# Column sums on TensorE against one column of ones instead of 64, at three places of a tuned transformer kernel

## The chip, the cores and the metric

The kernel runs as one program on one core of a Trainium2 chip. The metric is the device time of one launch in microseconds, as the median of several runs. Lower is better.

## What is computed

A sequence of 512 tokens of width 1024 goes through three layers. Layer A mixes tokens with a gated delta net of six heads of 128, and also attends to a memory of 256 rows; layer B has stick-breaking attention of twelve heads in that place; layer C pools, does a difference of two softmax attentions for four heads, and a cross attention to a second memory. Each layer ends with an MLP of width 4096. The change touches three sums of squares inside the layers:

```python
q = l2norm(qkv[..., :W].reshape(B, S, H, Dh)) * (Dh ** -0.5)      # layer A, six heads
k = l2norm(qkv[..., W:2 * W].reshape(B, S, H, Dh))                # layer A, six heads
...
o = o * lax.rsqrt(jnp.mean(o * o, axis=-1, keepdims=True) + EPS) * o_gain      # layer A, six heads
...
o = rms_norm_2(o, g_subln[l]) * (1.0 - lam_init)                  # layer C, four heads of 128
```

Each is one number per token and head: the sum of 128 squares.

## The kernel before, in words

Activations lie transposed: a head is a tile of 128 partitions (its features) by 512 tokens. A weight matrix comes in units of 1024 by 256 from DMA into `STG`, and ScalarE and VectorE split each unit into a high and a low part (`WH`, `WL`). TensorE multiplies high by high, high by low and low by high; these are the rows `HH,WH`, `HL,WH` and `HH,WL` of the profile. All engines follow an order written out by hand and meet through counting semaphores. TensorE's order is the function `_(pe)`, and every matmul of its helper `mm` shows as line 500.

A sum of squares over a head goes like this. ScalarE squares the head's tile (into `SQ`, or into `KDC`, which lies in the buffer `Y`). TensorE takes a block of 128 tokens of the squares as the stationary operand and streams columns of ones through it; the result in PSUM has the 128 tokens on partitions, and each streamed column gives the same sum. With `[:, 0:64]` the sum is written 64 times side by side, and the next block's result starts one column further and writes over 63 of them. In the end the columns from the first one on hold one sum per block, and VectorE reads only those.

The three places:

- `beside_gate(n)`, n from 0 to 5, lies between and behind the two tiles of each of three gate units of layer A. Each call does two of the twelve heads of queries and keys, four blocks each. Heads 0 to 5 of its order go to columns from 0 of PSUM bank 6, heads 6 to 11 to columns from 256. VectorE reads them at lines 2518 (`decays_2`) and 2540 (`decays_4`).
- `norm_sums(g, bank)` does three heads of the delta net's output, twelve blocks. `norm_sums(0, 7)` lies in the triangular inversion of the second group of heads (`between_1`, step 1), `norm_sums(1, 4)` beside the output projection of layer A (`norms_beside`).
- `head_sums(h)` in `out_between_heads` does one head of layer C, four blocks: one call ahead of `tile_k(0)` of the output projection, three behind it.

Other sums of the kernel, in `sum_tokens`, have the same form with one column of ones:

```python
mm(PS[:, 4, b:b + 1], blk(SQA[:, :], b), con("ones")[:, 0:1], b == 0, False, skip_group_check=True)
```

At four places between layers, `finish_post` runs two and then five matmuls whose results nobody reads (`keep_running`, rows `WH`), one set ahead of `spread_tokens` and one behind it.

Of the kernel before, what the change touches and what calls it, by code (L numbers as in the profile page):

```python
# [27 lines left out]
ALU = mybir.AluOpType  # L28
# [3 lines left out]
P = 128  # L32
# [3 lines left out]
NB = S // P  # L36
# [6 lines left out]
EPS = 1e-6  # L43
# [70 lines left out]
def program(nc, ws, xt_in, memt_in, memt2_in, par_in, con_in, rope_in, rcnt_in, out):  # L114
    ctx = ExitStack()
    with ctx:
        def sb(name, shape, dt=F32, scope=ctx, align=32):
            return scope.enter_context(nc.sbuf_tensor(name, shape, dt, align_bytes=align))
# [15 lines left out]
        SC = sb("SC", [P, H_LIN, 8, NB])  # L134
# [15 lines left out]
        SQ = sb("SQ", [P, 4, S])  # L150
# [9 lines left out]
        PS = ctx.enter_context(nc.psum_tensor("PS", [P, 8, 512], F32))  # L160
        PSF = PS[:, :, :].rearrange("p b n -> p (b n)")

        def con(name, width=P):
            return CON[:, CCOL[name]:CCOL[name] + width]
# [84 lines left out]
        KDC = [Y[:, 3 + e, :] for e in range(3)]  # L249
# [30 lines left out]
        def blk(ap, b, n=P):  # L280
            return ap[:, b * n:(b + 1) * n]
# [35 lines left out]
        def emptied(kind, u, j, i=None, step=0):  # L317

            return lin(EMPTIED[kind][u] + j + 1, 2 * step, i)
# [20 lines left out]
        def split_done(q, k):  # L340
            return 8 * SPLITS.index(q) + k + 1
# [154 lines left out]
        def _(pe):  # L496
            I_ = con("ident")

            def mm(o, l, r, start, stop, **kw):
                return pe.matmul(o, l, r, start=start, stop=stop, **kw)  # L500
# [26 lines left out]
            def wait_bank(u, j, i=None, step=0):  # L527

                if u >= 2:
                    kind = KIND[u - 2]  # L530
                    pe.wait_ge(sems[f"emptied_{kind}"], emptied(kind, u - 2, j, i, step))
# [494 lines left out]
            def norm_sums(g, bank):  # L1026

                pe.wait_ge(sems["osq"], 3 * g + 6)
                for e in range(3):
                    for b in range(NB):  # L1030
                        last = mm(PS[:, bank, NB * e + b:NB * e + b + 64], blk(KDC[e], b), con("ones")[:, 0:64], True, True)
                last.then_inc(sems["oss"], 1)

            def norm_rows(n, bank):
# [6 lines left out]
            def norms_beside(n):  # L1041
                if n == 1:
                    norm_sums(1, 4)
                if n == 3:
                    norm_rows(3, 2)
                    norm_rows(4, 3)
                    norm_rows(5, 4)
# [185 lines left out]
            def out_between_heads(u):  # L1233

                def tile_k(k):
                    pe.wait_ge(sems["hl"], split_done("C.mix", k))
                    for j in range(2):
                        bank = PS[:, 2 * (u % 2) + j, :]
                        wh, wl = WH[u % 2][:, k, j * P:(j + 1) * P], WL[u % 2][:, k, j * P:(j + 1) * P]
                        mm(bank, wh, HH[:, k, :], k == 0, False)  # L1240
                        mm(bank, wh, HL[:, k, :], False, False)
                        last = mm(bank, wl, HH[:, k, :], False, k == KD - 1)
                        if k == KD - 1:
                            last.then_inc(sems["tile"], 1)

                def head_sums(h):
                    pe.wait_ge(sems["df_sq"], h + 1)
                    for b in range(NB):
                        last = mm(PS[:, 7, NB * h + b:NB * h + b + 64], blk(SQ[:, h, :], b), con("ones")[:, 0:64], True, True)
                    if h == 3:  # L1250
                        last.then_inc(sems["df_ss"], 1)

                def head_factors(h):
                    for b in range(NB):
                        last = mm(PS[:, 4 + h, b * P:(b + 1) * P], COEF[:, NB * h + b:NB * h + b + 1].to_broadcast([P, P]),
                                  I_, True, True)
                    last.then_inc(sems["df_bc"], 1)

                pe.wait_ge(sems["emptied_act"], emptied("act", U0["C.mem"] + 7, 1))
                pe.wait_ge(sems["df_at"], 12)  # L1260
                pe.wait_ge(sems["lo"], u + 1)
                wait_bank(u, 0)
                wait_bank(u, 1)
                head_sums(0)
                tile_k(0)
                head_sums(1)
                head_sums(2)
                head_sums(3)
                tile_k(1)
                tile_k(2)  # L1270
                pe.wait_ge(sems["df_rs"], 3)
                head_factors(0)
                head_factors(1)
                tile_k(3)
                head_factors(2)
                head_factors(3)
                for k in range(4, KD):
                    tile_k(k)
# [26 lines left out]
            def beside_gate(n):  # L1305

                for t in (2 * n, 2 * n + 1):
                    pe.wait_ge(sems["l2sq"], t + 1)
                    if t == 6:
                        pe.wait_ge(sems["sc_dve"], 7)  # L1310
                    for b in range(NB):
                        c = NB * t + b if t < 6 else 256 + NB * (t - 6) + b
                        last = mm(PS[:, 6, c:c + 64], blk(SQ[:, t % 4, :], b), con("ones")[:, 0:64], True, True)
                    last.then_inc(sems["l2ss"], 1)
                if n == 0:
                    pe.wait_ge(sems["emptied_dve"], emptied("dve", U0["A.bg"], 1))
                    for b in range(NB):
                        last = pe.transpose(PS[:, 5, b * 12:(b + 1) * 12], blk(BGT[0:12, :], b), I_[0:12, 0:12])
                    last.then_inc(sems["bg_tr"], 1)
                if n == 3:  # L1320
                    mm(PS[:, 5, 64:88], con("tri_le"), SC[:, :, 0, :], True, True)
                    mm(PS[:, 5, 96:120], con("ones"), SC[:, :, 0, :], True, True).then_inc(sems["gc_mm"], 1)
                if n == 4:
                    pe.wait_ge(sems["rows_in"], 4)
                    pe.wait_ge(sems["sc_dve"], 10)
                    pe.wait_ge(sems["sc_act"], 7)
                    for ty in range(3):
                        last = pe.transpose(PS[0:64, 5, P + ty * P:2 * P + ty * P], ROWS_IN[:, ty, :], I_)
                    last.then_inc(sems["rows_tr"], 1)
# [5 lines left out]
            for r in range(NU["A.gate"]):  # L1335
                product(U0["A.gate"] + r, None, 0, HH, HL, between=lambda: beside_gate(2 * r),
                        beside=lambda n: memory_a(16 * r + n))
                beside_gate(2 * r + 1)
# [721 lines left out]
        def _(dve):  # L2060
# [3 lines left out]
            def tt(o, a, b, op):  # L2064
                return dve.tensor_tensor(o, a, b, op)  # L2065
# [418 lines left out]
            hb = lambda ap: ap.rearrange("p (h b) -> p h b", b=NB)  # L2484
            sm = [SMALL[:, r, :] for r in range(8)]
            step_ = [0]

            def sc(ins):

                step_[0] += 1  # L2490
                ins.then_inc(sems["sc_dve"], 1)
                dve.wait_ge(sems["sc_dve"], step_[0])
# [22 lines left out]
            def decays_2():  # L2515

                dve.wait_ge(sems["l2ss"], 6)
                sc(dve.tensor_scalar(sm[6], PS[:, 6, 0:24], EPS, None, ALU.add))
                sc(dve.reciprocal(sm[6], sm[6]))
                sc(tt(hb(sm[2]), SC[:, :, 1, :], hb(sm[6]), ALU.mult))  # L2520
                row = ROWS_IN[:, 2, :].rearrange("p (a n) -> p a n", a=2)[:, :, 0:24]
                dve.tensor_copy(row, sm[2].unsqueeze(1).to_broadcast([P, 2, 24])).then_inc(sems["rows_in"], 1)
# [14 lines left out]

            def decays_4():
                dve.wait_ge(sems["l2ss"], 12)
                sc(dve.tensor_scalar(SC[:, :, 3, :], hb(PS[:, 6, 256:280]), EPS, P * P * EPS, ALU.add, ALU.mult))  # L2540

            def gate_tile(u, i, step, j):
                t = 2 * (u - U0["A.gate"]) + j
# [4 lines left out]
            for r in range(NU["A.gate"]):  # L2548
# [17 lines left out]
                if r == 1:  # L2566
                    rows()
            decays_4()
            delta_net()
            for q, k in enumerate((3, 4, 5)):  # L2570
# [313 lines left out]
```

## Time and profile before

| what | value |
|---|---|
| runs of the kernel | 2172.91, 2175.64, 2178.26 us |
| median | 2175.64 us |
| time of the profiled execution | 2172.91 us |
| its span in the trace | 2171.1 us |
| granted TensorE clock, mean | 0.997 |
| TensorE matmul busy | 2110.8 us, 97% of the span |
| TensorE weight load busy | 1738.7 us, 80% |
| VectorE / ScalarE / GpSimd busy | 1082.4 / 746.4 / 178.9 us |
| DMA | 182.81 MB, 84 GB/s on average |

The span runs from the first to the last instruction; the profiled execution's own time is 1.8 us longer. PE is TensorE's matmuls, PEld its weight loads, which run ahead of the matmuls and beside them. The matmuls are pipelined, so their times overlap: the cost of a matmul in a row of many is the distance from its start to the next one's start, and not its duration. One fp32 matmul of the code appears as two matmuls with a weight load each in the trace; they are called passes here.

### The profile page before, as it was taken

How to read it: one execution, taken by the hardware profiler on the slowest of the kernel's cores; microseconds unless marked ns; L12 is line 12 of the kernel's file. 1: busy time of each engine (PE TensorE's matmuls, PEld its weight loads, DVE VectorE, ACT ScalarE, POOL GpSimd, SP SyncE). 2: the span in 40 equal slices, each digit the busy share in tenths (PEclk: the TensorE clock that was granted, in tenths of full speed). 3: DMA queues.
4: the chain of work that ended last, by engine and by line, in shares of the span. 5: the costliest groups of instructions: out<-in, count | busy, mean ns of one | idle time of the engine just before them, and what ended most of it. 6: DMA issues, size and time to landing. Idle time of an engine off the chain costs nothing.

```text
span 2171.1 us, 28830 instructions
## 1 busy us (share of the span) xinstructions
PE 2110.8 (97%) x11847; PEld 1738.7 (80%) x11847; DVE 1082.4 (50%) x1381; ACT 746.4 (34%) x1025; POOL 178.9 (8%) x145
## 2 busy tenths in 40 slices
PE   7999999999999999999999999999899999999998
PEld 7887788788888878767788888788688878888886
DVE  4764655455354453353645445455675345354453
ACT  6444433422122232574412222322464243222221
POOL 3000220300000220001300000311001000000001
PEclk9999999999999999999999999999999999999999
DMA  6231000232322222101222222232132202222221
GB/s 242 78 116 41 21 22 4 77 112 87 105 96 85 107 77 86 39 1 59 78 97 97 97 97 97 107 117 97 59 119 96 84 33 97 97 97 97 97 97 58
DMA packets 27025, 182.81 MB, mean 84 GB/s; under 512 B 2992, under 2 KB 3120, under 8 KB 5424
## 3 DMA queue, kind: packets, MB, share of 16 engines
q1 hardware_dynamic: 25776, 177.67, 23.2%
q0 software_dynamic: 432, 2.62, 0.3%
q8 instruction: 74, 1.21, 0.2%
q10 hardware_dynamic: 720, 1.11, 0.1%
q14 instruction: 23, 0.19, 0.0%
HBM read 179.30 MB, written 2.10 MB: 84 GB/s over the span
## 4 chain that ended last, share of the span: by engine, by line
PE 89%; DVE 6%; ACT 4%; DMA 1%; issue 1%; ACTq 0%; DVEq 0%
PE PS L500 88%; ACT Y L1389 2%; DVE Y L2062 1%; ACT WH L1389 1%; DVE WL L2065 1%; DVE Y L2065 1%; DMA MX<-mem_t 0%; DVE SQ L2065 0%; DMA STG<-weights 0%; PE PS L713 0%; DVE DMX L2676 0%; ACT ABUF L1389 0%; DVE HL L2065 0%; DVE HL L2062 0%; ACT SQ L1389 0%
## 5 line engine op out<-in xcount | busy, mean ns | idle before, releaser
L500 PE MATMUL PS<-HH,WH 128*128 128x512 f32 (+1 forms) x1608 | 631.7, 393 | 9.1 <-ACT HH L1389 4.3
L500 PE MATMUL PS<-HH,WL 128*128 128x512 f32 (+1 forms) x1608 | 619.9, 386 | 0.0
L500 PE MATMUL PS<-HL,WH 128*128 128x512 f32 (+1 forms) x1608 | 609.1, 385 | 0.0
L2065 DVE TENSOR_TENSOR WL<-STG,WH 128x2048 fp32r<-128x2048 f32 (+1 forms) x163 | 367.9, 2257 | 284.7 <-ACT WH L1389 284.6
L1389 ACT ACTIVATE WH<-STG 128x2048 fp32r<-128x2048 f32 (+2 forms) x171 | 314.9, 1841 | 523.8 <-PE PS L500 521.9
L500 PEld LDWEIGHTS PS<-HH,WH 128*128 128x128 f32 x1608 | 302.2, 188 | 85.3 <-issue 12.9
L500 PEld LDWEIGHTS PS<-HL,WH 128*128 128x128 f32 x1608 | 302.2, 188 | 61.4 <-issue 2.4
L500 PEld LDWEIGHTS PS<-HH,WL 128*128 128x128 f32 x1608 | 302.3, 188 | 59.5
L500 PE MATMUL PS<-UPH,WH 128*128 128x512 f32 x832 | 324.3, 390 | 1.4 <-DVE UPL L2062 1.4
L500 PE MATMUL PS<-UPH,WL 128*128 128x512 f32 x832 | 323.8, 389 | 0.0
L500 PE MATMUL PS<-UPL,WH 128*128 128x512 f32 x832 | 323.8, 389 | 0.0
L500 PEld LDWEIGHTS PS<-UPH,WH 128*128 128x128 f32 x832 | 156.2, 188 | 34.0 <-DVE UPL L2062 1.8
L500 PEld LDWEIGHTS PS<-UPL,WH 128*128 128x128 f32 x832 | 156.2, 188 | 32.4
L500 PEld LDWEIGHTS PS<-UPH,WL 128*128 128x128 f32 x832 | 156.2, 188 | 32.4
L423 POOL TENSOR_TENSOR SQA<-SQ 128x512 f32<-128x512 f32 (+1 forms) x14 | 24.2, 1728 | 1571.7 <-ACT SQ L1389 1571.7
L2062 DVE SCALAR_TENSOR_TENSOR RR<-PS,RS 128x512 f32<-128x512 f32 x96 | 66.3, 691 | 146.3 <-PE PS L500 138.4
L2065 DVE TENSOR_TENSOR Y<-Y,PS 128x512 f32<-128x512 f32 x64 | 44.0, 688 | 180.1 <-PE PS L500 180.1
L1389 ACT ACTIVATE UPH<-RR 128x512 fp32r<-128x512 f32 x64 | 40.5, 632 | 226.7 <-DVE RR L2062 226.7
L2065 DVE TENSOR_TENSOR XT<-XT,PS 128x512 f32<-128x512 f32 x80 | 54.7, 684 | 122.0 <-PE PS L500 121.8
L427 POOL TENSOR_TENSOR SQA<-SQA,SQ 128x512 f32<-128x512 f32 (+1 forms) x70 | 99.4, 1420 | 145.2 <-ACT SQ L1389 141.6
L1389 ACT ACTIVATE Y<-PS 128x512 f32<-128x512 f32 (+5 forms) x96 | 61.5, 645 | 82.1 <-PE PS L500 67.7
L2065 DVE TENSOR_TENSOR RQ<-RR 128x512 f32<-128x512 f32 x96 | 66.5, 692 | 3.3
(286 smaller groups left out, 2005.1 us busy)
## 6 DMA issues: line engine op xcount, KB each, us to landing
STG<-weights SPq DMA_DIRECT2D x163, 1024.0 KB, 4.8
XT<-x_t SPq DMA_DIRECT2D x2, 1024.0 KB, 9.0
out_t<-Y SPq DMA_DIRECT2D x8, 256.0 KB, 2.0
STG<-weights SPq DMA_DIRECT2D x4, 256.0 KB, 5.7
MX<-mem_t ACTq DMA_DIRECT2D x4, 256.0 KB, 7.7
CON<-consts SPq DMA_DIRECT2D x1, 1024.0 KB, 8.8
Y<-recip_counts POOLq DMA_DIRECT2D x1, 1024.0 KB, 5.0
KVM<-mem_t POOLq DMA_DIRECT2D x1, 1024.0 KB, 7.0
```

The source lines that it names most:

```text
L423: pool.tensor_tensor(SQA[:, 0:n], SQ[:, base % 4, 0:n], SQ[:, (base + 1) % 4, 0:n], ALU.add).then_inc(sems["sqa"], 1)
L427: pool.tensor_tensor(SQA[:, 0:n], SQA[:, 0:n], SQ[:, (base + k) % 4, 0:n], ALU.add).then_inc(sems["sqa"], 1)
L500: return pe.matmul(o, l, r, start=start, stop=stop, **kw)
L1389: return act.activation(o, i, f, **kw)
L2062: return dve.scalar_tensor_tensor(out=o, in0=a, scalar=s_, in1=b, op0=op0, op1=op1)
L2065: return dve.tensor_tensor(o, a, b, op)
```

## The change

At the three places the ones have one column, `con("ones")[:, 0:1]`, and the result in PSUM is one column wide. In bank 6 heads 6 to 11 of `beside_gate` now go to columns 0 to 23 and heads 0 to 5 to columns 24 to 47, and the two reads of VectorE follow. The number of instructions, their order, the stationary operands, and all waits and signals stay.

```diff
--- before.py
+++ after.py
@@ -1028,7 +1028,7 @@
                 pe.wait_ge(sems["osq"], 3 * g + 6)
                 for e in range(3):
                     for b in range(NB):
-                        last = mm(PS[:, bank, NB * e + b:NB * e + b + 64], blk(KDC[e], b), con("ones")[:, 0:64], True, True)
+                        last = mm(PS[:, bank, NB * e + b:NB * e + b + 1], blk(KDC[e], b), con("ones")[:, 0:1], True, True)
                 last.then_inc(sems["oss"], 1)
 
             def norm_rows(n, bank):
@@ -1246,7 +1246,7 @@
                 def head_sums(h):
                     pe.wait_ge(sems["df_sq"], h + 1)
                     for b in range(NB):
-                        last = mm(PS[:, 7, NB * h + b:NB * h + b + 64], blk(SQ[:, h, :], b), con("ones")[:, 0:64], True, True)
+                        last = mm(PS[:, 7, NB * h + b:NB * h + b + 1], blk(SQ[:, h, :], b), con("ones")[:, 0:1], True, True)
                     if h == 3:
                         last.then_inc(sems["df_ss"], 1)
 
@@ -1309,8 +1309,8 @@
                     if t == 6:
                         pe.wait_ge(sems["sc_dve"], 7)
                     for b in range(NB):
-                        c = NB * t + b if t < 6 else 256 + NB * (t - 6) + b
-                        last = mm(PS[:, 6, c:c + 64], blk(SQ[:, t % 4, :], b), con("ones")[:, 0:64], True, True)
+                        c = NB * ((t + 6) % 12) + b
+                        last = mm(PS[:, 6, c:c + 1], blk(SQ[:, t % 4, :], b), con("ones")[:, 0:1], True, True)
                     last.then_inc(sems["l2ss"], 1)
                 if n == 0:
                     pe.wait_ge(sems["emptied_dve"], emptied("dve", U0["A.bg"], 1))
@@ -2515,7 +2515,7 @@
             def decays_2():
 
                 dve.wait_ge(sems["l2ss"], 6)
-                sc(dve.tensor_scalar(sm[6], PS[:, 6, 0:24], EPS, None, ALU.add))
+                sc(dve.tensor_scalar(sm[6], PS[:, 6, 24:48], EPS, None, ALU.add))
                 sc(dve.reciprocal(sm[6], sm[6]))
                 sc(tt(hb(sm[2]), SC[:, :, 1, :], hb(sm[6]), ALU.mult))
                 row = ROWS_IN[:, 2, :].rearrange("p (a n) -> p a n", a=2)[:, :, 0:24]
@@ -2537,7 +2537,7 @@
 
             def decays_4():
                 dve.wait_ge(sems["l2ss"], 12)
-                sc(dve.tensor_scalar(SC[:, :, 3, :], hb(PS[:, 6, 256:280]), EPS, P * P * EPS, ALU.add, ALU.mult))
+                sc(dve.tensor_scalar(SC[:, :, 3, :], hb(PS[:, 6, 0:24]), EPS, P * P * EPS, ALU.add, ALU.mult))
 
             def gate_tile(u, i, step, j):
                 t = 2 * (u - U0["A.gate"]) + j
```

## Rows read from the trace of the kernel before

**Rows 1.** The page: busy time by engine, and the chain that ended last.
```profile
PE 2110.8 (97%) x11847; PEld 1738.7 (80%) x11847; DVE 1082.4 (50%) x1381; ACT 746.4 (34%) x1025; POOL 178.9 (8%) x145
...
PE 89%; DVE 6%; ACT 4%; DMA 1%; issue 1%; ACTq 0%; DVEq 0%
```

**Rows 2.** Groups by line, shapes kept apart, TensorE: busy us, mean ns of one.
```profile
L500 PE MATMUL PS<-CON,SQ 128*128 128x64 f32 x128 | 15.4, 273 | 0.0
...
L500 PE MATMUL PS<-CON,SQA 128*128 128x1 f32 x104 | 12.4, 238 | 0.0
...
L500 PE MATMUL PS<-CON,Y 128*128 128x64 f32 x48 | 5.7, 275 | 0.0
```

**Rows 3.** TensorE in order of time, 64-column blocks and what follows: start us, us.
```profile
190.53 1.89 PE L500 MATMUL PS<-CON,SQ 128*128 128x64 f32 x16
192.26 0.61 PE L713 MATMUL PS<-CON,Y 128*128 128x128 f32 x4
...
225.59 2.00 PE L500 MATMUL PS<-CON,SQ 128*128 128x64 f32 x16
227.52 0.73 PE L500 MATMUL PS<-ROWS,IND 64*128 64x512 f32 x2
...
302.12 2.89 PE L500 MATMUL PS<-CON,Y 128*128 128x64 f32 x24
304.94 0.68 PE L500 MATMUL PS<-Y,SQ 64*64 64x64 f32 x16
...
1634.08 2.79 PE L500 MATMUL PS<-CON,SQ 128*128 128x64 f32 x24
1636.67 0.48 PE L500 MATMUL PS<-HH,WH 128*128 128x512 f32 x1
```

**Rows 4.** The chain that ended last, in order of time, around one block.
```profile
302.12 6.77 PE PS L500 x152
```

**Rows 5.** TensorE in order of time, blocks of one column and of 128 columns.
```profile
1818.17 0.95 PE L500 MATMUL PS<-CON,SQA 128*128 128x1 f32 x8
1818.98 1.03 PE L500 MATMUL PS<-CON,SQ 128*128 128x1 f32 x8
1819.88 0.49 PE L500 MATMUL PS<-UPH,WH 128*128 128x512 f32 x1
...
1639.51 1.95 PE L500 MATMUL PS<-CON,DST 128*128 128x128 f32 x16
1641.21 0.48 PE L500 MATMUL PS<-HH,WH 128*128 128x512 f32 x1
```

**Rows 6.** Weight loads in order of time, ahead of blocks of 64 and of one column.
```profile
355.83 0.19 PEld L500 LDWEIGHTS PS<-HH,WH 128*128 128x128 f32 x1
356.06 0.19 PEld L500 LDWEIGHTS PS<-HL,WH 128*128 128x128 f32 x1
...
356.51 2.87 PEld L500 LDWEIGHTS PS<-CON,Y 128*128 128x128 f32 x24
359.30 0.19 PEld L500 LDWEIGHTS PS<-HH,WH 128*128 128x128 f32 x1
...
1818.95 0.97 PEld L500 LDWEIGHTS PS<-CON,SQ 128*128 128x128 f32 x8
1819.85 0.19 PEld L500 LDWEIGHTS PS<-UPH,WH 128*128 128x128 f32 x1
```

**Rows 7.** Instructions by tile: duration ns min/median/max, first and last start.
```profile
L500 PE MATMUL PS<-CON,SQ x96: 217/275/323, 166.7 to 227.3; 128*128 128x64 f32 x96
...
L500 PE MATMUL PS<-CON,SQA x104: 164/250/251, 30.6 to 2158.9; 128*128 128x1 f32 x104
```

**Rows 8.** Stretches: PE, PEld, DVE, ACT, POOL busy (instructions), granted clock, DMA share, GB/s.
```profile
298.00:300.00 2.00, 0.90 (x24) 0.65 (x20) 2.00 (x6) 0.01 (x1) 2.00 (x4) 1.00 0.00 0
302.00:304.00 2.00, 2.00 (x18) 1.89 (x17) 0.06 (x1) 0.11 (x1) 2.00 (x4) 1.00 0.00 0
...
768.00:770.00 2.00, 1.83 (x5) 0.92 (x3) 1.84 (x3) 0.69 (x2) 2.00 (x2) 0.50 0.00 0
```

**Rows 9.** TensorE in order of time, the same work at full and at lowered clock.
```profile
407.48 1.16 PE L500 MATMUL PS<-CON,RSC 128*128 128x128 f32 x8
408.40 1.40 PE L500 MATMUL PS<-WH 128*128 128x512 f32 x5
411.19 0.47 PE L500 MATMUL PS<-HH,WH 128*128 128x512 f32 x1 [1.40 <-ACT HH L1389]
...
766.36 1.34 PE L500 MATMUL PS<-CON,RSC 128*128 128x128 f32 x8
767.35 2.48 PE L500 MATMUL PS<-WH 128*128 128x512 f32 x5
770.18 0.67 PE L500 MATMUL PS<-HH,WH 128*128 128x512 f32 x1 [0.34 <-ACT HH L1389]
```

## The prediction

> **What bounds the kernel now.** I read the page first, for the engine that sets the time. TensorE's matmuls are busy for 97% of the span and hold 89% of the chain that ended last [rows 1]. The next engine, VectorE, is busy half of the time. So work taken from TensorE's stream of matmuls shortens the kernel nearly one for one, and the question is whether this change takes any.
>
> Next I read the groups by line with the shapes kept apart, to find the instructions that the change touches. They are the groups with 64 columns: 128 passes on SQ and 48 on Y, 176 in all [rows 2]. The code has 24 matmuls in each half of the queries and keys, so 48; twice 12 in `norm_sums`; and four times four in `head_sums`. That is 88, and two passes each give 176. The group with one column, on SQA, belongs to `sum_tokens` and stays; it shows what the changed instruction looks like in this kernel.
>
> The mean duration of a pass, 273 to 275 ns, is no price, since passes overlap. The price is the distance from start to start, so the third view is TensorE in order of time. The 176 passes stand there in ten blocks: six of 16 in `beside_gate`, two of 24 in `norm_sums`, one of 8 and one of 24 in `head_sums`. From the start of a block to the start of what follows: 192.26 - 190.53 = 1.73 us for 16; 227.52 - 225.59 = 1.93 us for 16, the longest of the six; 304.94 - 302.12 = 2.82 us for 24; 1636.67 - 1634.08 = 2.59 us for 24 [rows 3]. That is 108 to 121 ns a pass. As bounds, ten blocks at these rates hold between 176 x 0.108 = 19.0 us and 176 x 0.121 = 21.3 us. This is the whole time at stake, under 1% of the span. The blocks do lie on the path: the chain in order of time runs through the block at 302.12 without a break [rows 4]. So nothing is hidden by another engine here. If a pass gets shorter, from start to start, the kernel gets shorter.
>
> **The change part by part.**
>
> *63 of 64 columns, 176 times.* What sets 108 to 121 ns a pass, the columns streamed or the weight load of 128 by 128 that stands ahead of each? The trace holds both comparisons. Blocks with one column: 8 and 8 passes one behind the other take 1819.88 - 1818.17 = 1.71 us. A block with 128 columns: 16 passes take 1641.21 - 1639.51 = 1.70 us. Both start behind a 512-column matmul and end at one [rows 5]. So 16 passes cost the same with one column as with 128, and 64 lies between. The weight loads say why: with 64 columns they start 359.30 - 356.51 = 2.79 us apart over 24, or 116 ns each with the first gap, in which the last 512-column matmul ahead still streams; with one column they start 1819.85 - 1818.95 = 0.90 us apart over 8, or 112 ns each [rows 6]. The loads of 512-column passes stand 356.06 - 355.83 = 0.23 us apart [rows 6]; with a first gap of that length taken out, the block of 24 gives 2.56 / 23 = 111 ns. A load every 111 to 112 ns with either width: the load sets the pace, and streaming the columns lies beside the next load. Value taken: 0 for each of the 176.
>
> Bounds for this term. The best block with one column has 8 passes from 1818.17 to 1818.98, 0.81 us or 101 ns each [rows 5]. If all 176 went from 111 to 101 ns, the gain would be 1.8 us; I take this as the lower end although that block owes its short time to its place behind a 512-column matmul. On the other side, 1.71 against 1.70 us allows 0.01 / 16 x 176 = 0.1 us of loss. I choose 0 because the block of 24 behind a 512-column matmul, 2.59 us or 108 ns a pass, already has the pace of 16 single columns, 1.71 us or 107 ns.
>
> *The end of each block.* The last pass of a block isn't followed by another load of its kind, and there its own length can count. The median duration is 275 ns with 64 columns and 250 ns with one; the shortest are 217 and 164 ns [rows 7]. So what waits for the block's result gets it 25 to 53 ns sooner. Ten blocks give at most 10 x 0.053 = 0.5 us. But at eight of the ten ends the next matmul's load starts in the cadence of the loads, and the last pass delays nobody. Two have a different follower with a gap ahead of it, the one at 225.59 and the one at 302.12: there 1.93 and 2.82 us [rows 3] are 0.14 and 0.13 us over 112 ns a pass. I count 25 to 50 ns for these two: 0.1 us gained, between 0 and 0.5.
>
> *The readers on VectorE and ScalarE* get their numbers some 25 ns sooner. TensorE doesn't wait for them soon: in all these places it goes on with other matmuls. Nothing is added there.
>
> *The new columns of bank 6.* VectorE reads 24 columns before and after, at another offset. The wait ahead of head 6 stays in its place. Cost 0; I see no row that would give it another sign.
>
> Sum: 0 for the passes, -0.1 us for the ends, against the profiled execution's 2172.91 us: 2172.8 us. That execution was the fastest of the three shown; the median is 2175.64 us, 2.7 us above it. The forecast for the median is 2175.64 - 0.1 = 2175.5 us.
>
> **The rivals.**
>
> *The streamed columns are paid in full.* If weight load and streaming didn't overlap, each pass would save the difference of the shortest durations, 217 - 164 = 53 ns, and 176 x 0.053 = 9.3 us would go: 2166.3 us, 0.43% faster. For it speaks only that the durations do differ. Against it: 16 passes with 128 columns, twice as many as here, take no longer than 16 with one [rows 5]. A chance of 3 in 100.
>
> *The clock falls.* Here the change is slower. The granted clock is 1.00 around the block at 302.12, in a stretch of small matmuls and waits, and 0.50 at 768 to 770 [rows 8], in work between two layers where the one-column sums of `sum_tokens` are followed by waits: 1.2 GHz in place of 2.4. The price of such a fall comes from the same work at either level: the five matmuls on WH take 2.48 in place of 1.40 us, the eight passes on RSC 1.34 in place of 1.16, the first projection matmul 0.67 in place of 0.47 [rows 9]. That is 1.08 + 0.18 + 0.20 = 1.5 us. Fewer streamed columns mean less activity in ten places. Against it: at 298 to 300 us TensorE was busy for 0.90 of 2.00 us and the clock stayed at 1.00 [rows 8], and a block lasts under 3 us between dense matmuls. One fall gives 2177.0 us, still within what can be told from no change. It decides from five falls on (5 x 1.5 = 7.5 us, 0.34%); one in each of the ten blocks gives 2190.5 us. I give one or two falls 5 in 100, and five or more 2 in 100. The Trainium skill, "TensorE: Matmul & The Clock Gate", Part 1, says that a monitor of how busy the array is gates its clock, and that half rate is the default state which activity releases. By that rule thinner matmuls in a thin stretch speak against this change. Here the trace agrees that the clock has two levels and that it fell in a stretch with waits; whether columns count as activity no row of before shows.
>
> *A wait takes the place of the passes.* If passes did get shorter, the matmuls behind a block could come early for their operand. This would eat the gain of the first rival and end at no change, 2175.5 us; it is part of the likeliest case.
>
> **How the numbers follow.** The likeliest case, weight loads set the pace, has 90 in 100, and its own range is that of the terms, -2.3 (1.8 + 0.5) to +0.1 us, widened by the spread of the three runs, which is 2.7 us below and 2.6 us above the median: 2170.6 to 2178.3 us. One or two falls of the clock reach to 2175.5 + 3.0 + 2.6 = 2181.1 us. I give 2170.5 to 2181.0 us; it leaves the far ends of the two rivals out, 5 in 100, and some of the scatter between runs and chips.
>
> About 0.3% (6.5 us) is what a measurement of this kernel can tell from no change. Faster than that: the first rival, 3 in 100, and 1 in 100 for a scatter of the medians. Slower: the clock, 2 in 100, and 1 in 100 for scatter. Within 0.3%: 93 in 100.
>
> **What would show it in the profile after.** The groups on CON,SQ and on CON,Y have one column, a mean of 240 to 252 ns in place of 273 to 275, and less busy time in sum. In order of time the blocks keep their length: 1.7 to 1.9 us for 16 passes, 2.6 to 2.8 us for 24; the weight loads in them stand 111 to 112 ns apart. The granted clock is 1.00 in all ten places. The prediction is wrong if a block of 16 falls by as much as 16 x 0.053 = 0.85 us, to 0.9 or 1.0 us, or if a stretch of 290 to 345 us shows a clock under 1.00.

## The result: slower by 0.7%

| kernel | runs | median us | lowest to highest | mean clock over the runs |
|---|---|---|---|---|
| before | 8 | 2174.18 | 2172.59 to 2178.26 | 0.997 (profiled execution only) |
| changed | 8 (clock: all 31 on record) | 2187.98 | 2183.74 to 2196.34 | 0.9876 (0.984 to 0.992) |

The ratio is 1.007, with a 95% interval of 1.0057 to 1.0083. (All ratios here are those on record; they lie nearer to the quotient of the means than to that of the medians, which is 1.0063 here.) The forecast was no change, 2175.5 us and at most 2181.0. The time is outside the range, and near the end of the rival named "the clock falls", which had 2190.5 us for one fall in each of the ten blocks.

The page of the changed kernel, busy time by engine and the chain that ended last:

```profile
span 2181.9 us, 28830 instructions
...
PE 2121.4 (97%) x11847; PEld 1747.8 (80%) x11847; DVE 1082.5 (50%) x1381; ACT 747.0 (34%) x1025; POOL 179.0 (8%) x145
...
PE 89%; DVE 6%; ACT 4%; DMA 1%; issue 1%; ACTq 0%; DVEq 0%
```

Beside [rows 1]: the same instructions, the same chain. Only TensorE got longer, by 10.6 us of matmuls, and the span by 10.8 us. VectorE, ScalarE and GpSimd are within 0.6 us of before. The profile page doesn't tell why; the groups of the changed instructions, kept apart by shape, come next (busy us, mean ns):

```profile
L500 PE MATMUL PS<-CON,SQ 128*128 128x1 f32 x232 | 29.0, 250 | 2.0 <-ACT SQ L1389 2.0
...
L500 PE MATMUL PS<-CON,Y 128*128 128x1 f32 x48 | 6.0, 258 | 0.0
```

The change was made: 128 passes joined the 104 one-column passes on SQ that were there, and the 48 on Y have one column; a mean of 250 (over all 232) and 258 ns in place of 273 and 275 [rows 2]. Then TensorE in order of time, blocks and what follows them:

```profile
167.21 1.84 PE L500 MATMUL PS<-CON,SQ 128*128 128x1 f32 x16
168.98 0.41 PE L1318 MATMUL PS<-CON,BGT 12*128 12x12 f32 x4
...
194.22 1.84 PE L500 MATMUL PS<-CON,SQ 128*128 128x1 f32 x16
195.92 0.63 PE L713 MATMUL PS<-CON,Y 128*128 128x128 f32 x4
...
229.28 1.95 PE L500 MATMUL PS<-CON,SQ 128*128 128x1 f32 x16
231.15 1.19 PE L500 MATMUL PS<-ROWS,IND 64*128 64x512 f32 x4
...
307.35 3.26 PE L500 MATMUL PS<-CON,Y 128*128 128x1 f32 x24
310.54 1.12 PE L500 MATMUL PS<-Y,SQ 64*64 64x64 f32 x16
...
364.78 2.73 PE L500 MATMUL PS<-CON,Y 128*128 128x1 f32 x24
367.37 0.58 PE L500 MATMUL PS<-HH,WH 128*128 128x512 f32 x1
367.75 0.63 PE L500 MATMUL PS<-HL,WH 128*128 128x512 f32 x1
368.17 0.63 PE L500 MATMUL PS<-HH,WL 128*128 128x512 f32 x1
```

The first block takes 168.98 - 167.21 = 1.77 us. The others are the same blocks as in [rows 3]: 195.92 - 194.22 = 1.70 us against 1.73; 231.15 - 229.28 = 1.87 us against 1.93; 367.37 - 364.78 = 2.59 us, and the same block took 359.33 - 356.74 = 2.59 us before. So the blocks themselves didn't lose. The lines of before for that block and for the first one of `beside_gate`:

```profile
166.66 1.89 PE L500 MATMUL PS<-CON,SQ 128*128 128x64 f32 x16
168.48 0.41 PE L1318 MATMUL PS<-CON,BGT 12*128 12x12 f32 x4
...
356.74 2.79 PE L500 MATMUL PS<-CON,Y 128*128 128x64 f32 x24
359.33 0.48 PE L500 MATMUL PS<-HH,WH 128*128 128x512 f32 x1
```

But the dense matmuls behind the last block stand 0.42 us apart (367.75 to 368.17) and take 0.63 us, where they stand 0.23 us apart at full clock. The block at 307.35 takes 3.19 us in place of 2.82, because the lowered clock begins inside it.

The stretches of 2 us at these places (columns as in [rows 8]; the last but two is the granted clock):

```profile
168.00:170.00 2.00, 2.00 (x16) 1.92 (x16) 0.73 (x2) 0.00 (x0) 0.00 (x0) 0.91 0.00 0
170.00:172.00 2.00, 2.00 (x8) 1.61 (x7) 0.00 (x0) 0.39 (x1) 0.00 (x0) 0.50 0.00 0
172.00:174.00 2.00, 2.00 (x8) 1.32 (x7) 0.00 (x0) 1.25 (x3) 0.00 (x0) 0.74 0.00 0
...
184.00:186.00 2.00, 2.00 (x6) 1.06 (x5) 0.00 (x0) 0.00 (x0) 0.00 (x0) 0.50 0.00 0
...
276.00:278.00 2.00, 2.00 (x12) 2.00 (x11) 0.00 (x0) 1.48 (x2) 0.00 (x0) 0.50 0.54 131
...
310.00:312.00 2.00, 2.00 (x31) 1.98 (x33) 0.00 (x0) 0.00 (x0) 0.00 (x0) 0.50 0.00 0
312.00:314.00 2.00, 2.00 (x42) 2.00 (x41) 0.75 (x2) 0.00 (x0) 0.00 (x0) 0.50 0.00 0
...
368.00:370.00 2.00, 2.00 (x6) 1.52 (x6) 0.23 (x1) 0.00 (x0) 0.00 (x0) 0.50 0.00 0
```

In the trace of before, the clock is 1.00 in all stretches from 50 to 760 us. Here it is at its lower level (1.2 GHz for 2.4) right behind the first and second block of `beside_gate`, from within `norm_sums(0)` on, and right behind `norm_sums(1)`. It is also lower at 276 us, where nothing was changed. The busy share says nothing of it: TensorE is "busy" for 2.00 of 2.00 us in each of these stretches. What the falls cost can be read from the start times of the same block in both traces: the first block of `beside_gate` starts 0.6 us later than before (167.21 for 166.66), ahead of any changed matmul; the last of the six starts 3.7 us later (229.28 for 225.59), `norm_sums(0)` 5.2 us later (307.35 for 302.12), `norm_sums(1)` 8.0 us later (364.78 for 356.74). The 1.5 us between 3.7 and 5.2 are the fall at 276 us, behind no changed block. The fall behind `norm_sums(1)` makes nearly all of the next step: the block of 24 in `head_sums` starts 9.4 us later (1643.52 for 1634.08). The span ends 10.8 us later, as the last sums of the kernel ran at the lower clock too. So some 7.3 of the 10.8 us (3.1 + 2.8 + 1.4) stand in or behind changed blocks, and the rest stands elsewhere.

### The profile page after: what moved, and what is told of

Read it like the earlier page. It is cut to its first block, busy times and chain, and to the rows that moved or that the text cites. A ratio compares the mean times of both kernels' runs of the same rounds, so it can differ in the third digit from the quotient of the medians.

```text
span 2181.9 us, 28830 instructions
## 1 busy us (share of the span) xinstructions
PE 2121.4 (97%) x11847; PEld 1747.8 (80%) x11847; DVE 1082.5 (50%) x1381; ACT 747.0 (34%) x1025; POOL 179.0 (8%) x145
## 4 chain that ended last, share of the span: by engine, by line
PE 89%; DVE 6%; ACT 4%; DMA 1%; issue 1%; ACTq 0%; DVEq 0%
PE PS L500 88%; ACT Y L1389 2%; DVE Y L2062 1%; ACT WH L1389 1%; DVE WL L2065 1%; DVE Y L2065 1%; DMA MX<-mem_t 0%; DVE SQ L2065 0%; DMA STG<-weights 0%; PE PS L713 0%; DVE HL L2062 0%; DVE DMX L2676 0%; ACT ABUF L1389 0%; DVE HL L2065 0%; DVE XT L2065 0%
```

## The experiments

Each kernel ran beside the kernel before on the same chip. Each run also gives its mean granted clock, rounded to three digits; the table has the mean of these over all runs of a kernel. The experiments came in four groups, each with runs of before of its own. The record names chip 14 for the first group, chip 1 for the second and the fourth, and chip 0 for the third; kernels are compared within a group.

| run | what | runs | median us | ratio to before (95%) | mean clock |
|---|---|---|---|---|---|
| before, first group | | 35 | 2175.89 | | 0.9942 |
| e1_layout | new columns in bank 6, 64 ones | 12 | 2177.91 | 1.0009 (0.9998 to 1.002) | 0.9938 |
| e2_gate | one column in `beside_gate` | 12 | 2182.27 | 1.003 (1.0016 to 1.0045) | 0.9898 |
| e3_norm | one column in `norm_sums` | 12 | 2180.49 | 1.0023 (1.0013 to 1.0032) | 0.9919 |
| e4_head | one column in `head_sums` | 12 | 2176.78 | 1.0004 (0.9994 to 1.0015) | 0.9941 |
| before, second group | | 28 | 2176.67 | | 0.9939 |
| e5_w32 | 32 columns everywhere | 12 | 2180.95 | 1.0017 (1.0004 to 1.0031) | 0.9924 |
| e6_w128 | 128 columns everywhere | 11 | 2174.27 | 1.0003 (0.9992 to 1.0014) | 0.9943 |
| e7_fill | one column, and added dense matmuls | 4 | 2197.93 | 1.0096 (1.0079 to 1.0112) | 0.9882 |
| e8_sumtok64 | before, `sum_tokens` with 64 too | 10 | 2177.09 | 1.001 (0.9998 to 1.0022) | 0.9950 |
| before, third group | | 23 | 2178.05 | | 0.9934 |
| e10_spread | one column in `beside_gate`, scattered | 5 | 2185.83 | 1.0038 (1.0025 to 1.0051) | 0.9896 |
| e11_swap | squares stream, ones stationary | 11 | 2174.29 | 0.9989 (0.998 to 0.9999) | 0.9944 |
| e12_change_again | the change | 6 | 2189.37 | 1.0057 (1.0037 to 1.0077) | 0.9875 |
| e13_gate_again | e2_gate | 12 | 2181.32 | 1.0023 (1.0009 to 1.0037) | 0.9900 |
| before, fourth group | | 23 | 2177.13 | | 0.9934 |
| e14_spread64 | e10_spread's order, 64 columns | 12 | 2176.55 | 0.9993 (0.9981 to 1.0005) | 0.9947 |
| e15_spread_again | e10_spread | 12 | 2184.42 | 1.0029 (1.0017 to 1.0041) | 0.9899 |

**Which part of the change, and is it the columns in the bank?** Four kernels, each with a part.

```diff
 e1_layout: the changed kernel, with
-                        last = mm(PS[:, 6, c:c + 1], blk(SQ[:, t % 4, :], b), con("ones")[:, 0:1], True, True)
+                        last = mm(PS[:, 6, c:c + 64], blk(SQ[:, t % 4, :], b), con("ones")[:, 0:64], True, True)
 and 64 columns in norm_sums and head_sums as before
 e2_gate: the changed kernel, 64 columns in norm_sums and head_sums
 e3_norm: the kernel before, one column in norm_sums
 e4_head: the kernel before, one column in head_sums
```

> The kernel before with the new columns in bank 6 (heads 6 to 11 at 0, heads 0 to 5 at 24) and the two reads of VectorE moved, all sums still against 64 ones. Theory (fewer streamed columns let TensorE's clock fall): no change from before, 2174 us, mean clock 0.996 to 0.997. Rival (the new columns or the order of the writes in the bank cost the time): 2188 us, as the whole change.

> One column of ones in beside_gate alone (96 of the 176 passes), 64 in norm_sums and head_sums. Theory of the clock: the two falls seen behind these blocks (near 170 and 184 us) come back, two to four of them at 1.5 to 2 us each, so 3 to 8 us over before: 2177 to 2182 us, mean clock 0.992 to 0.994. Rival (one place alone makes all of the loss, the inversion): 2174 us here.

> One column of ones in norm_sums alone (48 passes). Theory of the clock: the falls near 309 to 316 us and at 368 us come back and nothing at 170 or 184 us; 5 to 9 us over before: 2179 to 2183 us, mean clock 0.992 to 0.994. Rival (the gate blocks make all of the loss): 2174 us here.

> One column of ones in head_sums alone (32 passes, 24 of them in one block). In the profile of the changed kernel no fall stands near 1640 us. Theory of the clock: 0 to 2 us over before, 2174 to 2176 us. Rival (each one-column pass costs time by itself, the same everywhere, 13.8 us over 176 passes, 78 ns each): 32 x 0.078 = 2.5 us, 2176.7 us, with longer blocks in the trace.

The layout alone shows no change: its interval holds 1. `beside_gate` alone loses 0.30% (6.4 us), `norm_sums` alone 0.23% (4.6 us), and the clock goes with it, 0.9898 and 0.9919. `head_sums` alone shows neither a loss nor a lower clock. So neither rival holds that puts all of the loss in one place; gate and norm together, 0.53%, carry most of the 0.57 to 0.7% of the whole. In the profile of e3_norm the gate stage keeps the clock, and the stretch with `norm_sums(0)` loses it:

```profile
160.00:240.00 80.00, 78.58 (x458) 57.01 (x456) 36.87 (x80) 36.23 (x92) 2.24 (x4) 1.00 0.14 50
...
300.00:320.00 20.00, 19.30 (x353) 18.11 (x353) 8.37 (x23) 3.92 (x12) 7.65 (x11) 0.74 0.01 2
```

In that of e2_gate it is the other way round:

```profile
160.00:240.00 80.00, 78.62 (x396) 56.73 (x396) 34.00 (x74) 35.35 (x91) 0.72 (x1) 0.94 0.12 45
...
300.00:320.00 20.00, 18.52 (x411) 16.86 (x411) 12.05 (x29) 3.86 (x13) 10.26 (x14) 1.00 0.01 3
```

**Does it go by width?** All ten blocks with 32, and with 128 columns, the columns in PSUM as before:

```diff
-  ... con("ones")[:, 0:64] ...
+  ... con("ones")[:, 0:32] ...     (e5_w32; 0:128 in e6_w128)
```

> The kernel before with 32 columns of ones in all ten blocks, columns in PSUM as before. Theory of the clock (it answers to the columns streamed in the blocks): between before and the change, some 2176 to 2184 us, mean clock between 0.996 and 0.988. Rival (only whether the result is one column wide counts, as a write narrower than some unit): 2175 us as before. Weight loads in the blocks stand 111 to 112 ns apart by both.

> The kernel before with 128 columns of ones in all ten blocks. Theory of the clock: the clock holds at least as well as with 64 columns, and as the loads still set the pace (16 passes of 128 columns took 1.70 us in the trace of before) no block is longer: 2173 to 2176 us, mean clock 0.996 to 0.998. Rival (the streamed columns are paid for): 176 passes x 27 ns more = 4.7 us, 2180 us.

With 32 columns the kernel is between before and the change, 1.0017 and clock 0.9924. The time has moved, if by little: the interval starts at 1.0004. The clock alone, 0.9924 against 0.9939, isn't clear of the scatter of the runs. As far as this goes, that the result is one column wide is not what counts, since 32 columns lose too. With 128 it is the same as before, 1.0003: the clock doesn't gain, and the added columns cost nothing. The block with 128 columns in TensorE's order of time:

```profile
190.79 1.95 PE L500 MATMUL PS<-CON,SQ 128*128 128x128 f32 x16
192.57 0.60 PE L713 MATMUL PS<-CON,Y 128*128 128x128 f32 x4
```

192.57 - 190.79 = 1.78 us for 16 passes, against 1.70 with one and 1.73 with 64. The weight load sets the pace from 1 to 128 columns; that step of the prediction stands, and 0.05 us over 64 columns is all that doubling them took in this block.

**Can the streamed columns be given back elsewhere in the block?** The changed kernel, and ahead of each four sums a matmul whose result nobody reads:

```diff
+                    mm(PS[:, bank, 256:512], con("ones"), CON[:, 0:256], True, True)
                     for b in range(NB):
                         last = mm(PS[:, bank, NB * e + b:NB * e + b + 1], blk(KDC[e], b), con("ones")[:, 0:1], True, True)
 and so in head_sums (bank 7) and beside_gate (bank 6)
```

> The changed kernel, one column of ones everywhere, and ahead of each four sums one matmul of 256 columns on constants whose result nobody reads: two passes of 256 columns, 512 columns against the 8 x 63 = 504 that the change took away, 22 such matmuls. Work is added, 44 passes at about 0.23 us = 10 us. Theory of the clock (activity of the array, wherever in the block it comes from): mean clock back to 0.995 to 0.997, 2175 + 10 = 2185 us, with few falls in the layer A mixer. Rival (one-column passes themselves, in number or form, bring the clock down): clock 0.988 as in the changed kernel, 2188 + 10 = 2198 us.

This is the rival's number: 2197.93 us, over four runs, with a clock of 0.9882 against 0.9939 of before in that group. The columns are back in number, and the clock isn't. TensorE in order of time shows what the experiment really did:

```profile
167.28 0.59 PE L500 MATMUL PS<-CON 128*128 128x256 f32 x2
167.71 0.95 PE L500 MATMUL PS<-CON,SQ 128*128 128x1 f32 x8
168.51 0.68 PE L500 MATMUL PS<-CON 128*128 128x256 f32 x2
169.03 0.95 PE L500 MATMUL PS<-CON,SQ 128*128 128x1 f32 x8
```

The filler stands beside the thin passes and not in place of them. The 8 passes of one column still take their 0.8 us (168.51 - 167.71), in which the array streams next to nothing. My wording, "activity of the array, wherever in the block it comes from", fell. What was left of the theory: the thin passes themselves count, and work added around them doesn't make up for it.

**One stretch, or the total?** First the sums of `beside_gate` were scattered, 40 of the 48 two passes at a time between the dense matmuls.

```diff
+            def beside_gate_step(p):
+                memory_a(p)
+                if p < 24:
+                    one_sum(p)
+                elif p >= 32:
+                    one_sum(p - 8)
...
-                        beside=lambda n: memory_a(16 * r + n))
+                        beside=lambda n: beside_gate_step(16 * r + n))
 one_sum(m): the two passes of block m % 4 of head m // 4, with the waits and the signal of beside_gate; sums 40 to 47 stay in beside_gate(5)
```

> One column of ones in beside_gate alone, as in e2_gate, but the sums no longer stand in blocks of 16 passes: 40 of the 48 sums stand singly (2 passes each) between the groups of dense matmuls of the gate units, the last 8 sums in one block as before. Same passes, same columns, same total. Theory (what brings the clock down is a stretch in which the array streams almost nothing, and it must be long in one piece): clock and time back to before, 2175 to 2177 us, few falls between 165 and 235 us. Rival (the total of thin passes counts, wherever they stand): as e13_gate_again beside it, 2180 to 2183 us, clock 0.990. A loss of up to 2 us by broken pipelining of the weight loads is possible in both.

> The kernel of e2_gate once more (one column in beside_gate alone, blocks of 16 passes), beside e10_spread on the same chip: 2180 to 2184 us, clock 0.990.

The theory said 2175 to 2177 us; measured were 2185.83 us with scattered sums (five runs) and 2181.32 us with blocks, at clocks of 0.9896 and 0.9900. Scattering 40 of the 48 sums didn't save the mean clock. As the new order could cost time by itself, the next two kernels part order and columns: the same order with 64 columns, beside the one-column kernel in one group.

```diff
-                last = mm(PS[:, 6, c:c + 1], blk(SQ[:, t % 4, :], b), con("ones")[:, 0:1], True, True)
+                last = mm(PS[:, 6, c:c + 64], blk(SQ[:, t % 4, :], b), con("ones")[:, 0:64], True, True)
```

> The order of e10_spread with 64 columns in the scattered sums of beside_gate: nothing differs from e15_spread_again beside it but the columns of 48 sums. If thin passes bring the clock down even when they stand two by two between dense matmuls (the total counts): clock back to 0.993 to 0.995 and 4 to 7 us less than e15_spread_again. If scattering alone had saved the clock and the order of e10_spread costs time by itself: no difference between the two.

> The kernel of e10_spread once more: 2183 to 2187 us, clock 0.989 to 0.992, if the first five runs stand.

With 64 columns the scattered order is as fast as before, 0.9993 and clock 0.9947; with one column 2184.42 - 2176.55 = 7.9 us slower, at 0.9899. The two kernels differ in the columns of 48 matmuls of the code and in nothing else. In order of time the sums cost the same in both; one column, then 64:

```profile
168.38 0.39 PE L500 MATMUL PS<-HH,WL 128*128 128x512 f32 x1
168.61 0.28 PE L500 MATMUL PS<-CON,SQ 128*128 128x1 f32 x2
168.75 0.48 PE L500 MATMUL PS<-HH,WH 128*128 128x512 f32 x1
```

```profile
170.55 0.40 PE L500 MATMUL PS<-HH,WL 128*128 128x512 f32 x1
170.79 0.33 PE L500 MATMUL PS<-CON,SQ 128*128 128x64 f32 x2
170.93 0.47 PE L500 MATMUL PS<-HH,WH 128*128 128x512 f32 x1
```

In both 0.14 us from the pair to the next dense matmul. So the columns alone make the 7.9 us. That the scattered pairs make them is not shown, and the profile of e15_spread_again speaks against it. Its last sums stand in one piece as before, 18 passes from 226.33 us on, and the clock by stretches, ahead of them and from them on, is:

```profile
226.33 2.17 PE L500 MATMUL PS<-CON,SQ 128*128 128x1 f32 x18
228.43 1.86 PE L500 MATMUL PS<-ROWS,IND 64*128 64x512 f32 x4
```

```profile
166.00:226.00 60.00, 60.00 (x299) 42.81 (x298) 26.11 (x60) 23.46 (x64) 0.00 (x0) 1.00 0.12 39
226.00:240.00 14.00, 14.00 (x72) 9.25 (x70) 3.45 (x8) 7.94 (x18) 0.73 (x1) 0.63 0.00 0
```

The clock is 1.00 over the whole stretch of the scattered pairs and falls right behind the piece that wasn't scattered; in the profile of e10_spread it does the same, and in that of e14_spread64, with 64 columns, it is 1.00 there too. The five profiles with one column and the blocks in one piece (the change twice, e2_gate, e13_gate_again and e7_fill) each have one to three falls in that stretch. So scattering may well have kept the clock where it was done, and the loss came from the last block and from falls further on. A kernel with these last eight sums scattered or widened would tell; there is none.

**And with no thin passes at all?** The operands change places in all ten blocks. The readers are left as they are and so take other numbers than the sums they should; this kernel is for its time only.

```diff
-                    for b in range(NB):
-                        last = mm(PS[:, bank, NB * e + b:NB * e + b + 64], blk(KDC[e], b), con("ones")[:, 0:64], True, True)
+                    last = mm(PS[:, bank, :], con("ones"), KDC[e], True, True)
 and so in head_sums and beside_gate
```

> In all ten blocks the operands change places: the ones are stationary (128 by 128) and the squares of a head stream through, 512 columns in 2 passes, in place of 8 passes of 64 columns. 22 such matmuls. The sums then lie along the free dimension, and the readers, left as they are, take other numbers than the sums they should: the output is not the reference's. The time of a head's sum is about 2 x 0.43 = 0.86 us against 8 x 0.112 = 0.90 us, and no thin stretch is left. Theory (thin stretches bring the clock down): clock at least that of before, 0.994 to 0.998, 2172 to 2176 us, with no falls behind the ten blocks. Rival (the clock falls near these places by the random look of it, whatever stands there): same number of falls as before or as the change.

0.9989, with an interval just below 1, and a clock of 0.9944 against 0.9934 of before in that group. The sums of two heads take 165.35 to 167.16, 1.81 us, in 4 passes:

```profile
165.35 1.88 PE L500 MATMUL PS<-SQ,CON 128*128 128x512 f32 x4
167.16 0.41 PE L1314 MATMUL PS<-CON,BGT 12*128 12x12 f32 x4
```

So 64 columns already had nearly all that dense work gives here. The falls that are left come from elsewhere: the profile of e11_swap has eight between 50 and 2160 us, and none behind one of the ten places. Widening `sum_tokens`, behind which two of them stand in its trace, didn't help either:

```diff
+            def sum_at(b, nt):
+                return PS[:, 4, b * P:b * P + 64] if nt == NB else PS[:, 4, b:b + 1]
-                    mm(PS[:, 4, b:b + 1], blk(SQA[:, :], b), con("ones")[:, 0:1], b == 0, False, skip_group_check=True)
+                    mm(sum_at(b, nt), blk(SQA[:, :], b), con("ones")[:, 0:64 if nt == NB else 1], b == 0, False, skip_group_check=True)
 and so for SQ; ScalarE's square root reads the sums 128 columns apart where nt is NB
```

> The kernel before, and sum_tokens too streams 64 columns of ones in place of one, where it has four blocks of tokens (13 places, 8 + 8 passes each), each token block to columns of its own. ScalarE reads the four sums 128 columns apart. Theory of the clock: the falls of before lie behind sum_tokens, at 766 and 1398 us in its trace; they become rarer, 0 to 4 us gained, 2171 to 2175 us, mean clock 0.997 to 0.999. Rival (these falls come from the waits in finish_post and not from the thin passes): 2175 us, clock as before.

1.001, with an interval that holds 1; the clock, 0.9950 against 0.9939, is the highest of the table, but no time came with it. In its one profile the falls at 766 and 1398 us are gone. That little came of it fits what the fall at 766 us cost. The profile of the change has none at that place, and the same work shows there at full clock:

```profile
775.97 1.16 PE L500 MATMUL PS<-CON,RSC 128*128 128x128 f32 x8
776.88 1.41 PE L500 MATMUL PS<-WH 128*128 128x512 f32 x5
779.60 0.47 PE L500 MATMUL PS<-HH,WH 128*128 128x512 f32 x1 [1.31 <-ACT HH L1389]
```

From start to start it takes 779.60 - 775.97 = 3.63 us, against 770.18 - 766.36 = 3.82 us at the lowered clock [rows 9]. TensorE waits for ScalarE there in both, 1.31 us at full and 0.34 us at the lowered clock, so the wait took up nearly all of the slower matmuls, and that fall cost 0.2 us.

The change once more, in the third group:

> The changed kernel once more, on the chip of these runs: 2184 to 2192 us, 0.7% over before, clock 0.986 to 0.990.

1.0057 (1.0037 to 1.0077) over 6 runs, clock 0.9875: the first result stands.

**Does the clock account for the whole loss?** At half clock for a time T, TensorE does T / 2 less work, and the mean clock of the span falls by T / (2 x span). Where TensorE sets the time, the lost T / 2 is added to the span, so that a mean clock lower by x costs about x times the span. In the third group the change has 0.9934 - 0.9875 = 0.0059 less, worth 0.0059 x 2175 = 12.8 us; the mean spans differ by 2187.8 - 2175.5 = 12.3 us. Scattered sums in the fourth group: 0.9947 - 0.9899 = 0.0048, worth 10.4 us; spans 2182.4 - 2174.9 = 7.5 us. This is an upper price, as a fall in a wait costs little (0.2 us at 766 us) and low clock counts in the mean wherever it stands. Over the 109 runs of before in the four groups the span grows by 1.05 us for each 0.001 of mean clock lost, about half of the 2.2 us of the formula. So the means alone allow the clock to be the whole loss, and don't prove it. The stronger evidence is the one pair of profiles above: the steps by which the change falls behind stand at the stretches of low clock.

## Why the prediction was wrong

*What bounds the kernel:* right. TensorE's stream is the time, 89% of the chain before and after, and so a slower TensorE was paid in full inside the layers, if not between them.

*63 of 64 columns, 176 times, at 0:* right. The blocks kept their length within 0.03 us where the clock was full (1.70 for 1.73, 2.59 for 2.59), and 128 columns cost almost nothing either (1.78 us).

*The end of each block, -0.1 us:* the block of 16 with a gap behind it took 1.87 us for 1.93, so 0.06 us were gained at this end. An end at which the prediction expected nothing gained as much: the first block of `beside_gate` took 1.77 for 1.82 us. The size is right and drowns in the rest.

*The new columns of bank 6, at 0:* right within the measurement, 1.0009 (0.9998 to 1.002).

*The clock:* this is the step that failed. The sum had no term for it, which is to price it at 0, and the case of five and more falls had 2 in 100. The runs showed a mean clock of 0.9876 in place of the 0.997 of the profile of before, and 11 to 14 us more. The mechanism was named, as a rival, and the experiments bear it out. Its price of 1.5 us a fall holds inside the layers: the two falls at 170 and 184 us cost 3.7 - 0.6 = 3.1 us over the gate stage, 1.6 us each. It doesn't hold at the place it was read from. There the prediction summed durations and left out the wait behind them; from start to start that fall cost 0.2 us. The time at ten falls, 2190.5 us, is 2.5 us from the median, and this is luck in part: the profile has low clock at four of the ten blocks, not at ten, and more at a place that wasn't changed and at the end. Three steps led to the 0.

- "At 298 to 300 us TensorE was busy for 0.90 of 2.00 us and the clock stayed at 1.00" was taken as proof that the places have room. One stretch of one execution shows that the clock can hold there, not that it does in every one. The mean clock of the profiled execution of before was 0.997; over the 35 runs of the first group it was 0.9942, from 0.990 to 0.998. The profile had shown one of the better draws, and the kernel before already lives with several falls a run. The spread of its three times, 2172.91 to 2178.26 us, was the hint: 5.35 us are three or four falls at 1.5 us. That time and mean clock scatter together, the 109 runs of before show (a correlation of -0.88).
- "A block lasts under 3 us between dense matmuls" supposed that a short block can't do it. In the profile of the change the clock falls right behind blocks of 1.8 us, at 170 and 184 us.
- The sum priced the columns by the time they take on TensorE, which is nothing, and then wrote "0". What they did besides, keep the clock up, was in the rival's paragraph and in no term of the sum.

The Trainium skill, "TensorE: Matmul & The Clock Gate", Part 1, calls the half rate the default, which activity releases. The prediction cited this as speaking against the change and set it aside; the runs agree with it, at clocks of 0.9875, 0.9924 and 0.9947 with 1, 32 and 64 columns (e12, e5 and e14, in three groups).

The predicted signs in the profile named the right place to look: the blocks kept their length, and a clock under 1.00 between 290 and 345 us was what would show it wrong.

*What stays open.* Falls also stand where nothing was changed. One place stands out, between 268 and 284 us: all seven profiles with one column in `beside_gate` have a fall there, and three of the nine others (e1_layout, e8_sumtok64, e11_swap). This points to thin passes that make a fall further on likelier too, and with one execution for each profile it is not shown; no mechanism for it is. Which blocks a fall stands behind isn't fixed either: e3_norm has low clock from 302 to 312 us and none behind `norm_sums(1)`, and the profile of the change has it behind both. And why `head_sums`, with one block of 24 between dense matmuls like `norm_sums(1)`, showed no loss (1.0004) isn't settled; a fall did stand right behind that block in the profiles of e4_head and e12_change_again, at 1641 and 1649 us.

## What to carry to other kernels

When an instruction's width costs no time, because a weight load sets the pace, it is not free to remove: on TensorE, whose clock fell here when the columns went, the idle columns may be what holds the clock. Read the mean clock of many runs, not of one profile, and take a scatter of a few us in a kernel of fixed work as a sign that the clock is near the edge; then price a thinner stream with the falls in the sum and not as a remote case. Ask too where a fall would stand: beside a wait it cost 0.2 us here, in a stage without one 1.6 us. A cheap test beforehand is a change of width in both directions: here 64, 128 and 512 columns were within 0.11% of before, and 32 and 1 were slower.

## What the runs showed of the hardware that was not expected

- One column in place of 64, with the same start-to-start times, costs through the clock: 7.9 us for the 48 sums of the scattered order. In its profiles the clock held over the stretch with single pairs between dense matmuls and fell behind the 18 passes in one piece.
- Dense filler beside thin passes didn't help: with 22 added matmuls of 256 columns the clock was 0.9882 over four runs, against 0.9876 for the change without them, in another group.
- A fall of the clock costs what the place makes of it: 1.6 us each at 170 and 184 us, 0.2 us at 766 us, where TensorE waits for ScalarE behind it.
- A matmul of fp32 with 512 streamed columns (2 passes, 0.9 us for a head) is as fast as 8 passes with a weight load each (0.9 us): 1.81 us for two heads, against 168.48 - 166.66 = 1.82 us before, and the clock is no lower (0.9944 against 0.9934).
- The end of the kernel, where TensorE has little left to do, runs at the lower clock in all profiles, from the stretch at 2162 us on in before. In the profile of the change it began a little earlier in the work, before TensorE's last 16 passes were done, and cost about 1 us.
